# The last 24 blocks of V read whole instead of gathered, in the expert stage of a hybrid decoder block

## The reference, cut to what matters

```
def peer_ffn(h, w_peer_q, peer_keys, peer_u, peer_v):
    q = (h @ w_peer_q).reshape(b, s, 8, 2, 128)
    sc = einsum('bshcd,hckd->bshck', q, peer_keys)
    s1, i1 = top_k(sc[..., 0, :], 16)            # first keys, 0..127
    s2, i2 = top_k(sc[..., 1, :], 16)            # second keys, 0..127
    cand_s = s1[..., :, None] + s2[..., None, :]
    cand_i = i1[..., :, None] * 128 + i2[..., None, :]
    top_s, pos = top_k(cand_s.reshape(..., 256), 16)
    eid = take_along_axis(cand_i.reshape(..., 256), pos)
    gate = softmax(top_s)
    act = gelu(einsum('bthkd,btd->bthk', peer_u[eid], h), approximate=False)
    return einsum('bthk,bthkd->btd', gate * act, peer_v[eid])
```

## Time and profile before

| | us |
|---|---|
| median of 3 runs | 2637.36 (2636.16 to 2637.39) |
| profiled execution, its own time | 2636.65 |
| its span, first to last instruction | 2635.0 |
| PE busy | 1685.6 (64%) |
| DVE busy | 1622.4 (62%) |
| ACT busy | 867.0 (33%) |
| POOL busy | 638.4 (24%) |
| software queue (all gathers), bytes | 549.49 MB |

### The profile page before, as it was taken

One profiled execution on the slowest core, in us unless ns is written; L12 is line 12 of the kernel. 1 busy time (PEld: TensorE's weight loads), 2 busy tenths in 40 slices (PEclk: granted clock), 3 DMA queues, 4 the chain that ended last, 5 costly groups with the idle time before them and its releaser, 6 DMA issues.

```text
span 2635.0 us, 29465 instructions
## 1 busy us (share of the span) xinstructions
PE 1685.6 (64%) x9753; PEld 1260.1 (48%) x9753; DVE 1622.4 (62%) x2480; ACT 867.0 (33%) x1738; POOL 638.4 (24%) x617
## 2 busy tenths in 40 slices
PE   7899999999999999999962222322232232223225
PEld 6798878888888888978960000000000000000001
DVE  5887637766767766775686766666654444444441
ACT  4466445545545445545442022201221101111000
POOL 1000000100001001040034644443443343333332
PEclk9799999999999999999986666666666566666666
DMA  5244556665665655556589999999999999999998
GB/s 181 81 152 141 168 159 196 199 190 167 194 189 174 192 186 181 174 189 219 197 339 419 420 420 420 420 420 420 420 420 420 420 420 421 420 420 420 420 420 325
DMA packets 211420, 774.26 MB, mean 294 GB/s; under 512 B 18968, under 2 KB 54160, under 8 KB 144016
## 3 DMA queue, kind: packets, MB, share of 16 engines
q0 software_dynamic: 75584, 549.49, 50.7%
q1 hardware_dynamic: 135264, 223.61, 27.4%
q10 hardware_dynamic: 496, 0.23, 0.0%
HBM read 771.09 MB, written 2.16 MB: 293 GB/s over the span
## 4 chain that ended last, share of the span: by engine, by line
PE 45%; DMA 37%; DVE 9%; issue 5%; POOL 2%; ACT 1%; DVEq 0%; POOLq 0%; ACTq 0%; SPq 0%
DMA u_slots<-in_peer_u_dram,eid 32%; PE accA L1624 5%; PE accA L1626 5%; PE accA L1625 5%; DVE u_slots L1481 4%; PE accB L1624 4%; PE accB L1626 4%; PE accB L1625 4%; DMA v_slots<-in_peer_v_dram,v_eid 4%; PE accB L1618 2%; PE accB L1616 2%; PE accB L1617 2%; PE small L1634 1%; DVE w_lo L1062 1%; PE pair_d L1616 1%
## 5 line engine op out<-in xcount | busy, mean ns | idle before, releaser
L1481 DVE CUSTOM_DVE_ANT_0 u_slots<-u_slots,h 128x2048 f32<-128x2048 f32 x256 | 586.3, 2292 | 519.7 <-DMA u_slots<-in_peer_u_dram,eid 494.3
L1062 DVE TENSOR_TENSOR w_lo<-w_raw,w_hi 128x1024 fp32r<-128x1024 f32 (+1 forms) x420 | 523.3, 1256 | 291.7 <-ACT w_hi L724 290.4
L724 ACT ACTIVATE w_hi<-w_raw 128x1024 fp32r<-128x1024 f32 (+1 forms) x420 | 442.1, 1057 | 422.7 <-PE accB L1626 139.6
L660 POOL DMA_INDIRECT u_slots<-in_peer_u_dram,eid x256 | 262.0, 1023 | 780.5 <-DVE dots L1481 523.4
L1951 PE MATMUL accA<-v_slots,weight 128*32 128x512 f32 x512 | 113.7, 1038 | 482.5 <-DMA v_slots<-in_peer_v_dram,v_eid 482.5
L1951 PE MATMUL small<-v_slots,weight 128*32 128x512 f32 x496 | 111.1, 1045 | 413.4 <-DMA v_slots<-in_peer_v_dram,v_eid 413.4
L684 POOL DMA_INDIRECT v_slots<-in_peer_v_dram,v_eid x252 | 271.3, 1076 | 110.8 <-issue 82.3
L1951 PEld LDWEIGHTS accA<-v_slots,weight 128*32 128x32 f32 x512 | 21.9, 158 | 550.7 <-issue 550.7
L1951 PEld LDWEIGHTS small<-v_slots,weight 128*32 128x32 f32 x496 | 21.2, 158 | 481.5 <-issue 481.5
L1035 ACT ACTIVATE gelu_s<-dots 32x4 f32<-32x4 f32 x256 | 52.9, 207 | 589.0 <-DVE dots L1481 586.1
L1616 PE MATMUL accB<-act_hi,w_hi 128*128 128x256 f32 x512 | 145.1, 283 | 2.1 <-ACT ya L890 1.1
(11 more groups left out here) (370 smaller groups left out, 3829.6 us busy)
## 6 DMA issues: line engine op xcount, KB each, us to landing
w_raw<-in_w_in_dram SPq DMA_DIRECT2D x168, 512.0 KB, 3.7
w_raw<-in_w_in_dram SPq DMA_DIRECT2D x128, 256.0 KB, 3.1
w_raw<-in_w_o_ssm_dram SPq DMA_DIRECT2D x64, 512.0 KB, 3.8
w_raw<-in_w_o_attn_dram SPq DMA_DIRECT2D x32, 512.0 KB, 4.5
w_raw<-in_w_out_dram SPq DMA_DIRECT2D x32, 512.0 KB, 4.4
w_raw<-in_w_peer_q_dram SPq DMA_DIRECT2D x32, 512.0 KB, 4.6
cum_row<-cum_dram POOLq DMA_DIRECT2D x8, 1024.0 KB, 7.5
w_raw<-in_w_uq_dram SPq DMA_DIRECT2D x8, 512.0 KB, 5.4
```

The source lines that it names most:

```text
L660: pool.indirect_dma_start(u_slots[:, n % U_RING, :], None, peer_u[0], bass.IndirectOffsetOnAxis(ap=eid[:, u, k:k + 1], axis=0)).then_inc(u ...
L724: act.activation(w_hi[:, slot, :, 0:w], w_raw[:, slot, :, 0:w], ACT.Copy).then_inc(hi_split, 1)
L1062: dve.tensor_tensor(w_lo[:, slot, :, 0:w], w_raw[:, slot, :, 0:w], w_hi[:, slot, :, 0:w].bitcast(F32), ALU.subtract).then_inc(lo_split, 1)
L1481: dve.tensor_tensor_reduce(slot, slot, h2[:, u // PH, :], 1.0, 0.0, ALU.mult, ALU.add, dots[:, u % 2, k:k + 1]).then_inc(u_free, 1)
```

## The change

The last `DENSE` = 24 blocks of V (first keys 104 to 127) are no longer gathered. They are loaded whole by SP, 24 loads of 1 MiB, into the four U slots after the last U gathers. The V gathers from number 8 on get a bounds check: rows above `LAST_GATHERED` are left out, the slot keeps what it had, and the share of such a pick is zero in the weights (`gm`, the gate where the first key is under 104, else 0).

The shares of the picks in those blocks are spread to a matrix `dense_w` (128 second keys x 24 blocks x 256 tokens). A tile's first keys, second keys and shares are transposed (`turn_picks`, copied by `take_picks`), and for each *lot* of 16 tokens DVE builds ones where a key equals a column number (`lot_ones`), multiplied by the share's upper part (fp32r) and by what is left of it. PE multiplies them, 32 products of 128x128 weights by 24 columns a lot (`lot_shares`), and ACT copies the result (`take_lot`). Then each block is multiplied by `dense_w` (`dense_half`, four fp32 products of 128x128 by 512 for each tile). The lots of the first tile run in units 11 to 14, those of the second after the last dots, before any product of a block.

The order changes with it. U runs ahead from V gather 132 on, four U gathers to one of V; V has four slots there, and U gets the other four from gather 152 on. All U gathers are issued before V gather 156. The first tile's gathered sums are merged after unit 10 to free A and B, and these hold the lots' results and then the blocks' sums, which are merged at the end.

```diff
+DENSE = 24
+LOT = 16
...
+            for b in range(DENSE):
+                if b < 4:
+                    sp.wait_ge(u_free, PK * UNITS - 8 + b + 1)
+                else:
+                    sp.wait_ge(vd_free, b - 3)
+                sp.dma_start(u_slots[:, b % 4, :], peer_v[0, (FIRST_DENSE + b) * NK:(FIRST_DENSE + b + 1) * NK, :]
+                             ).then_inc(vd_landed[b % 4], 16)
...
+                elif n >= V_RING:
+                    pool.wait_ge(v_free, (n - (4 if V_LAST + 4 <= n < V_LATE + 4 else V_RING)) // 4 + 1)
...
-                                        bass.IndirectOffsetOnAxis(ap=v_eid[:, u, m // 4, m % 4:m % 4 + 1], axis=0)
+                                        bass.IndirectOffsetOnAxis(ap=v_eid[:, u, m // 4, m % 4:m % 4 + 1], axis=0),
+                                        bounds_check=LAST_GATHERED if n >= V_RING else NK * NK - 1, oob_is_err=False
...
+                elif n < V_LATE:
+
+                    ahead = V_LAST + 4 + LEAD + 4 * (n - V_LAST - 3)
+                else:
+                    ahead = PK * UNITS
...
+                act.activation(gelu_t[:, u, :], dots[:, u % 2, :], ACT.Gelu)
...
+            def take_lot(j):
+                act.wait_ge(g_full, j + 1)
+                act.activation(dense_w[:, :, j * LOT:(j + 1) * LOT],
+                               A[:, j % 2, 0:LOT * DENSE].rearrange("p (t b) -> p b t", b=DENSE),
+                               ACT.Copy).then_inc(g_taken, 1)
...
+            def lot_ones(j):
+
+                lot = slice(j % LOTS_T * LOT, (j % LOTS_T + 1) * LOT)
+                if j % LOTS_T == 0:
+                    dve.wait_ge(picks_turned, j // LOTS_T + 1)
+                    steps.mark(dve.tensor_tensor(share_lo[:, :], A[:, 0, 2 * P:3 * P], share_hi[:, :].bitcast(F32),
+                                                 ALU.subtract))
+                if j >= 2:
+                    dve.wait_ge(g_full, j - 1)
+                hi, lo = one_first[:, j % 2, 0, :, :], one_first[:, j % 2, 1, :, :]
+                steps.mark(dve.tensor_tensor(lo, iota[:, FIRST_DENSE:NK].unsqueeze(1).broadcast_to([P, LOT, DENSE]),
+                                             keys_p[:, 0, lot].unsqueeze(2).broadcast_to([P, LOT, DENSE]), ALU.is_equal))
+                dve.tensor_tensor(one_second[j % 2][:, :, :], iota[:, :].unsqueeze(1).broadcast_to([P, LOT, NK]),
+                                  keys_p[:, 1, lot].unsqueeze(2).broadcast_to([P, LOT, NK]), ALU.is_equal)
+                steps.wait()
+                step(dve.tensor_tensor(hi, lo.bitcast(F32),
+                                       share_hi[:, lot].bitcast(F32).unsqueeze(2).broadcast_to([P, LOT, DENSE]), ALU.mult))
+                dve.tensor_tensor(lo, lo.bitcast(F32),
+                                  share_lo[:, lot].bitcast(F32).unsqueeze(2).broadcast_to([P, LOT, DENSE]),
+                                  ALU.mult).then_inc(ones_ready, 1)
...
+            def lot_shares(j):
+
+                pe.wait_ge(ones_ready, j + 1)
+                if j >= 2:
+                    pe.wait_ge(g_taken, j - 1)
+                for i in range(LOT):
+                    for k in range(2):
+                        ins = pe.matmul(A[:, j % 2, i * DENSE:(i + 1) * DENSE], one_second[j % 2][:, i, :],
+                                        one_first[:, j % 2, k, i, :], start=k == 0, stop=k == 1)
+                ins.then_inc(g_full, 1)
+
+            def dense_half(i):
+
+                b, t = i // 2, i % 2
+                if i == 0:
+                    pe.wait_ge(g_taken, LOTS)
+                if t == 0:
+                    pe.wait_ge(vd_landed[b % 4], (b // 4 + 1) * 16)
+                for c in range(4):
+                    ins = pe.matmul(((A, B), (small, pair_d))[t][c // 2][:, c % 2, :], dense_w[:, b, t * P:(t + 1) * P],
+                                    u_slots[:, b % 4, c * BANK:(c + 1) * BANK],
+                                    start=t == 0 and b == 0, stop=t == 0 and b == DENSE - 1)
...
+            for n in range(0, V_LATE, 4):
+                v_group(n)
+                if n == V_LAST + 4:
+                    turn_picks(0)
+                j = (n - V_LAST - 8) // 4
+                if 0 <= j < LOTS_T // 2:
+                    lot_shares(2 * j)
+                    lot_shares(2 * j + 1)
+            turn_picks(1)
+            v_group(V_LATE)
+            late = V_LATE + 4
+            for j in range(LOTS_T, LOTS):
+                lot_shares(j)
+                if j % 2 and j < LOTS - 1:
+                    v_group(late)
+                    late += 4
+            groups = (PK * UNITS - 4 - late) // 4
+            for i in range(groups):
+                v_group(late + 4 * i)
+                for k in range(2 * DENSE * i // groups, 2 * DENSE * (i + 1) // groups):
+                    dense_half(k)
+            v_group(PK * UNITS - 4)
```

More of the change, by code:

```diff
@@ L381, in hybrid_block @@
         summed = sem("summed")
+        folded = sem("folded")
+        valued = sem("valued")
+        picks_full = sem("picks_full")
+        picks_turned = sem("picks_turned")
+        ones_ready = sem("ones_ready")
+        g_full = sem("g_full")
+        g_taken = sem("g_taken")
+        vd_landed = [sem(f"vd_landed{i}") for i in range(4)]
+        vd_free = sem("vd_free")
+        first_summed = sem("first_summed")
         stored = sem("stored")
@@ L591, in _ @@
                 steps.mark(select(past[:, b * P:(b + 1) * P], [[1, P]], 0, -1, NEG))
[L592 removed]
+            steps.mark(pool.tensor_copy(iota[:, :], iota_i[:, :]))
             steps.wait()
@@ L1025, in spread_gates @@
                 if u >= 2:
-                    act.wait_ge(weighed, u - 1)
+                    act.wait_ge(shared, u - 1)
                 for lanes, tokens, g, picks in spread_blocks():
-                    act.activation(gm_s[lanes, u % 2, :, g], gate[tokens, u, picks], ACT.Copy)
+                    act.activation(gm_s[lanes, u % 2, :, g], gm[tokens, u, picks], ACT.Copy)
             def unit_gelu(u):
@@ L1468, in top_experts @@
                 for u in range(n):
-                    for c in range(2):
-                        steps.mark(dve.tensor_reduce(part[:, c, u, :], (cand, pick)[u][:, c, :, :], AX.X, ALU.add))
+                    for c, of in enumerate((first, second)):
+                        steps.mark(dve.tensor_reduce(of[:, units[u], :], (cand, pick)[u][:, c, :, :], AX.X, ALU.add))
                 between()
                 wait()
-                dve.scalar_tensor_tensor(eid[:, all_units, :], part[:, 0, 0:n, :], float(NK), part[:, 1, 0:n, :],
+                dve.scalar_tensor_tensor(eid[:, all_units, :], first[:, all_units, :], float(NK), second[:, all_units, :],
                                          ALU.mult, ALU.add).then_inc(unit_ids, n)
@@ L1937, in _, with turn_picks @@
             key_scores(3)
[L1940 to L1957 removed]
+            def turn_picks(t):
+                pe.wait_ge(valued, t + 1)
+                if t == 0:
+                    pe.wait_ge(folded, 2)
+                else:
+                    pe.wait_ge(g_taken, LOTS_T)
+                for c, of in enumerate((first, second, gelu_t)):
+                    ins = transpose_to(A[:, 0, c * P:(c + 1) * P],
+                                       of[:, t * PH:(t + 1) * PH, :].rearrange("p u k -> p (u k)"))
+                ins.then_inc(picks_full, 1)
@@ new lines, in v_group @@
+            def v_group(n):
+                u, q = n // PK, n % PK // 4
+                t, h = u // PH, u % PH
+                if q == 0:
+                    pe.wait_ge(weighed, u + 1)
+                for g in range(4):
+                    pe.wait_ge(*v_landing(n + g))
+                for c in range(4):
+                    ps = ((A, B), (small, pair_d))[t][c // 2]
+                    for g in range(4):
+                        ins = pe.matmul(ps[g * GROUP:(g + 1) * GROUP, c % 2, :], weight[:, u % 2, q, g, :],
+                                        v_slot(n + g)[:, c * BANK:(c + 1) * BANK],
+                                        start=h == 0 and q == 0, stop=h == PH - 1 and q == 3)
+                    if n == PK * UNITS - 4:
+                        ins.then_inc(summed, 1)
+                if n < PK * UNITS - 4:
+                    ins.then_inc(v_free, 1)
```

203 lines of the change are left out of this document (135 added, 68 removed).

## The result

The changed kernel takes 2669.01 us (median of 4 runs, 2661.20 to 2674.13) against 2637.38 before: ratio 1.0118, 95% interval 1.0105 to 1.0131, slower by 32 us where 11 less was forecast. The profiled execution took 2674.13 us with a span of 2672.5, so the span forecast as 2623.5 came out 49 us longer.

What follows compares the result with a forecast made beforehand. It took TensorE to bound the first half and transfers the expert stage, with TensorE taking over after the last U gather. 2317 + 67 + 236 = 2620, plus 3.4 tail and 1.65 and 0.7, gave 2626 us; range 2612 to 2640.

Steps and rivals of the forecast that it cites:

- X: Time at which the last gather of U has landed, forecast at 2317 us.
- piece 1 of the sum: Time until the last gather of U has landed: 2304 us by bytes, 2317 with three additions.
- The cover: With U ahead, four gathers, 10 us, still queued behind a group of 5.6 to 6.8 us would hide POOL's standing.
- DVE's 47.2 of 48.0 us: From U gather 152 on, DVE's work per 16 U and 4 V gathers was just hidden by their transfers.
- POOL's wait: POOL stands at a V gather until TensorE has read the group before; 3 us taken together with DVE.
- uneven rows: Randomly dropped rows load the 16 DMA engines unevenly over V gathers 0 to 155: 7 to 18 us, 10 taken.
- my two maps of lanes: A DMA engine serves 8 neighbouring partitions or every 16th; fullest engine 23 or 58 rows above the mean.
- Piece 2: From the last U landing until the last share is spread, bound by TensorE's order of work: 67 us, bounds 46 to 92.
- the two rivals on the clock: During second-half lots, TensorE's clock stays full (2613 us, chance 0.17) or lots fall to half (2650 us, chance 0.20).
- Piece 3: The remaining 21 groups and 48 half blocks, bound by TensorE at full clock: 236 us.
- the 61 us: Net saving of 24.4 MiB at 2.50 us each, if the transfers stayed the bound to the end.
- The rival that ends slower: Second-half lots at half clock and groups slower too: 20.4 us a turn, 91 us for four, 2650 us; chance 0.20.

Runs made afterwards that it cites:

- grouped run: The changed kernel, whole, but from V gather 132 on POOL issues 16 U gathers, then four V gathers together; 2650.56 us.
- the fixed mask: The kernel before, with the same four lanes of every 32 dropped from the V gathers of units 2 to 15; 2638.04 us.
- the changing one: The kernel before, with four lanes of every 32 dropped from V gathers of units 2 to 15, the lanes changing with the unit; 2574.15 us.

## Why the prediction was wrong

**The step that failed: X, piece 1 of the sum.** I took 3 us for DVE and for POOL's standing at a V gather "with four gathers, 10 us, still queued behind a group of 5.6 to 6.8 us". X came 31 us later. The cover failed: POOL stood up to 9.4 us at a V gather, and behind it the transfers fell to 352 GB/s. POOL had issued late itself, as its issues took 1.9 us on average beside a DVE that was busy four fifths of the time, not the 1.07 of the earlier trace rows. What the runs show in its place: taking the standing away (four V gathers together) brings X 21 us forward in the traces, and the end 18 us by the medians; the order alone, without anything else of the change, loses 15 before X, of which grouping gives only 5 back. The two terms that I had weighed apart, DVE's 47.2 of 48.0 us and POOL's wait, act together: leaving out the lots gives 13 us in the traces (8 by the medians), but once POOL no longer stands they cost, with the drops, 2.4 us from 2100 to 2300 us.

**The drops.** The packets of the software queue stayed at 75584, and the bytes fell to 498.81 MB as forecast. 10 us were taken for uneven rows; 13 follow from the run that only drops. The sign and size held, my two maps of lanes behind it did not, so that the size came out near is luck. Of the 31 us, 7 remain (31 - 21 - 3). The grouped run has them in its first 100 us with U ahead: 2000 to 2100 us at 385 GB/s, 8 us behind the full rate. What slows this stretch, in every run with the new order (380 to 398), is open.

**Piece 2.** Group 156 starts 8.8 us after X (9 forecast). The four turns of a group and two lots take 17.7, 17.7, 14.5 and 14.5 us, 64.3 in place of 57.2. A pair of lots takes 11.3 and 11.6 us in the first two turns and 8.7 and 9.1 in the last two, 6 us more in all than four times my 8.7. TensorE was busy 11.10 of 11.10 us in the first pair with the clock at 0.62:

```profile
2363.30:2374.40 11.10, 11.10 (x68) 11.10 (x64) 4.10 (x5) 0.49 (x1) 4.04 (x4) 0.62 0.74 266
```

The forecast lay between the two rivals on the clock, and the truth lies between it and the slow one. The Trainium skill's rule ("TensorE: Matmul & The Clock Gate", Part 1), that activity releases the gate, does not by itself give this row: the engine is busy throughout and has the full clock in a quarter of it.

**Piece 3.** TensorE is the bound, at full clock, as forecast: busy 211.6 of 214 us. The size was 12 us off. A half block takes 3.54 us (1.82 to the start of the products into the next tensor and 1.72 to the end of those) where I had put 3.41, which is 6 us for 48; the groups take 3.57 and not 3.44, 3 us, and the first, partly at half clock, 1.4 more; the rest is short waits.

**The dense loads.** The last two U gathers land 3.7 us apart (2344.23 and 2347.96 above), not 2.5. In the run of the order alone, which loads no blocks, the last two dots start 2.5 us apart (2377.96 and 2380.44), each after waiting 0.2 us for its gather. So the blocks took their share in front of X. That agrees with the Trainium skill ("DMA: Bandwidth & Descriptors", Issuing engines are not separate DMA queues), by which such transfers interleave on the same engines.

**Where the 61 us went.** 31 before X, and behind X TensorE's 73 + 248 us, in which the transfers could have moved the 100 MiB that were left in 250 us at 420 GB/s, or in 272 at the 386 of the V-only stretch, a rate that the prediction did not have. The rival that ends slower named the lots' clock and 2650; slower lots gave 6 us. The larger loss, in the order of U and V, was no rival of mine: it stood in the sum at 3 us.

## What to carry to other kernels

An engine that issues transfers in order and waits in one ring stops all rings: give the short ring's gathers together, behind enough of the long ring's, so that the wait has passed when they come (18 us here by the medians). A cover that is 98% full and a wait that leans on the same queue are not two free terms; price the stretch as late. Work added to a stage bound by transfers should go where the other engines idle: here TensorE was idle 70% of the 900 us up to 2300, and most of the added work stood in the 320 us behind X, so halving the lots' products (20 us) and fewer blocks (5 us) decided the sign.

## What the runs showed of the hardware

- A stretch of gathers of which every second had 96 or 112 partitions in place of 128 ran at 229 GB/s, against 420, with the DMA share at 1.01.
- A row dropped by the bounds check costs 0.03 us at the most, but 12.5% of the lanes dropped always in the same places gained at most 4 of 70 us in three patterns, and 64 when the places changed from unit to unit.
- The DMA share of 0.99 did not show that: it stays near 1 while the bytes fall, as waiting engines show long packets (the slowest hundredth 0.95 us against 0.32). The GB/s column did.
- 128x128 weight loads with 24 columns behind them left TensorE's clock at 0.61 to 0.83 with the engine busy all the time.
- POOL's indirect issue takes 0.90 to 1.01 us where no operation of DVE over 0.5 us runs beside it, and 0.90 to 3.1 where one does, in all 18 traces. What counts is where the issue falls: from 1700 to 2400 us V's took 1.10 us on average with the fixed mask and 1.67 with the changing one, though DVE's dots took 321 and 340 us.
